# Two-layer hybrid trunk on one core: weight units rounded earlier, two low parts moved from GpSimd to VectorE, GpSimd's scalings moved behind two more units

## The reference

```python
def mixer_ab(h, w_in, ...):                      # layer 0
    u = h @ w_in                                 # pool | z | xbc | dt
    xbc = silu(causal_dwconv(xbc, conv_w) + conv_b)      # 4 taps
    ...                                          # chunked scan, gate with silu(z), norm
    return concat([pool_out, y]) @ w_out

def mixer_cd(h, w_in, dw_w, dw_b, ln_g, ln_b, sc_w, w_out):   # layer 1
    u = h @ w_in                                 # a | gate | bg | cg | hh, 1024 channels each
    v = u[a] * sigmoid(u[gate])
    v = causal_dwconv(v, dw_w) + dw_b            # 31 taps, 1024 channels
    conf_out = silu(layernorm(v) * ln_g + ln_b)
    sc_out = u[bg] * causal_dwconv(u[cg] * u[hh], sc_w)       # 3 taps
    return concat([conf_out, sc_out]) @ w_out
```

## Time and profile before

| | us |
|---|---|
| median of 3 runs | 904.92 |
| lowest, highest | 904.24, 906.71 |
| profiled execution, its own time | 906.82 |
| its span, first to last instruction | 905.1 |

### The profile page before, as it was taken

How to read it: one execution, slowest core, us unless ns; L and a number is a source line. 1 busy time by engine, 2 the same in 40 slices (tenths; PEclk the granted TensorE clock), 3 DMA queues, 4 the chain that set the end, 5 groups by cost and what they waited for, 6 DMA issues and landing times.

```text
span 905.1 us, 14746 instructions
## 1 busy us (share of the span) xinstructions
PE 877.0 (97%) x6078; PEld 801.9 (89%) x6078; DVE 622.7 (69%) x961; ACT 477.7 (53%) x697; POOL 176.0 (19%) x163
## 2 busy tenths in 40 slices
PE   8999998999999999999998999999999899999997
PEld 7899986899889999999898999787999799999996
DVE  4786996596576655555589999966587475555554
ACT  6664564565465544444564443357575555444443
POOL 1120710000000000000009888667200000000000
PEclk9999999999999999999999999999999999999999
DMA  8454434553455555665565676344552456565551
GB/s 294 146 179 147 136 103 155 167 185 120 149 179 187 189 187 194 193 191 187 185 178 168 197 216 195 126 150 155 183 164 93 141 186 211 189 192 195 190 188 70
DMA packets 82954, 155.27 MB, mean 172 GB/s; under 512 B 6838, under 2 KB 8776, under 8 KB 82888
## 3 DMA queue, kind: packets, MB, share of 16 engines
q1 hardware_dynamic: 82776, 154.29, 53.4%
q10 hardware_dynamic: 112, 0.05, 0.0%
HBM read 152.11 MB, written 1.05 MB: 169 GB/s over the span
## 4 chain that ended last, share of the span: by engine, by line
PE 74%; DVE 14%; ACT 4%; DMA 2%; POOL 2%; SPq 1%; issue 1%; DVEq 0%; POOLq 0%; ACTq 0%
PE ps L557 13%; PE ps L558 13%; PE ps L559 13%; PE ps L624 10%; PE ps L626 10%; PE ps L625 10%; DVE w_lo L1544 4%; ACT w_hi L1120 2%; DVE ps L1901 2%; DVE cv L2080 1%; DVE xT L1823 1%; POOL w_lo L2204 1%; DMA raw<-in_ab_w_in 1%; DVE h_lo L1555 1%; DVE xc L1611 1%
## 5 line engine op out<-in xcount | busy, mean ns | idle before, releaser
L1120 ACT ACTIVATE w_hi<-raw 128x1024 fp32r<-128x1024 f32 x284 | 295.1, 1054 | 220.9 <-DMA raw<-in_mlp_w 128.7
L1544 DVE TENSOR_TENSOR w_lo<-raw,w_hi 128x1024 fp32r<-128x1024 f32 x238 | 286.9, 1227 | 125.7 <-ACT w_hi L1120 124.9
L557 PE MATMUL ps<-h_hi,w_hi 128*128 128x256 f32 x1120 | 316.1, 282 | 10.4 <-POOL w_lo L2204 6.0
L558 PE MATMUL ps<-h_lo,w_hi 128*128 128x256 f32 x1120 | 313.9, 280 | 0.0
L559 PE MATMUL ps<-h_hi,w_lo 128*128 128x256 f32 x1120 | 313.7, 280 | 0.0
L557 PEld LDWEIGHTS ps<-h_hi,w_hi 128*128 128x128 f32 x1120 | 212.3, 190 | 13.8 <-POOL w_lo L2204 6.7
L559 PEld LDWEIGHTS ps<-h_hi,w_lo 128*128 128x128 f32 x1120 | 213.7, 191 | 0.0
L558 PEld LDWEIGHTS ps<-h_lo,w_hi 128*128 128x128 f32 x1120 | 212.0, 189 | 0.6
L2233 POOL TENSOR_TENSOR rfac<-stat,mhalf 128x1 f32<-128x1 f32 (+2 forms) x18 | 15.7, 872 | 624.5 <-DVE stat L1797 507.0
L2204 POOL TENSOR_TENSOR w_lo<-raw,w_hi 128x1024 fp32r<-128x1024 f32 x46 | 114.7, 2517 | 23.4 <-ACT w_hi L1120 23.4
L624 PE MATMUL ps<-w_hi,r_hi 128*128 128x512 f32 x256 | 99.8, 390 | 0.0
(11 more groups left out here) (274 smaller groups left out, 1237.7 us busy)
## 6 DMA issues: line engine op xcount, KB each, us to landing
raw<-in_mlp_w SPq DMA_DIRECT2D x128, 512.0 KB, 3.8
raw<-in_cd_w_in SPq DMA_DIRECT2D x40, 512.0 KB, 4.0
raw<-in_xa_wkv SPq DMA_DIRECT2D x32, 512.0 KB, 3.8
raw<-in_ab_w_in SPq DMA_DIRECT2D x24, 512.0 KB, 4.6
raw<-in_xa_wq SPq DMA_DIRECT2D x16, 512.0 KB, 3.6
raw<-in_xa_wo SPq DMA_DIRECT2D x16, 512.0 KB, 3.8
raw<-in_cd_w_out SPq DMA_DIRECT2D x16, 512.0 KB, 3.6
raw<-in_ab_w_out SPq DMA_DIRECT2D x12, 512.0 KB, 3.7
```

The lines of the kernel that those rows point to most:

```text
L557: nc.tensor.matmul(dst, wt[0], x[0], start=start, stop=False, skip_group_check=True)
L558: nc.tensor.matmul(dst, wt[0], x[1], start=False, stop=False, skip_group_check=True)
L1120: nc.scalar.activation(w_hi[:, v % SLOTS, :, :], raw[:, v % SLOTS, :, :], ACT.Copy)\
L1544: V.tensor_tensor(w_lo[:, v % SLOTS, :, :], raw[:, v % SLOTS, :, :], f(w_hi[:, v % SLOTS, :, :]), ALU.subtract).then_inc(lo_ready_dve, 1)
```

## The change

Four edits, all to the order of work or to who does it; nothing that is computed changes.

1. `pool_lo` begins two units later: the low parts of units 148 and 149 go from GpSimd to VectorE.
2. ScalarE rounds unit 7 ahead of the first taps of the 4-tap convolution, and VectorE takes its low part ahead of `conv4(0)` and no longer inside it.
3. ScalarE rounds units 18 and 19 each ahead of a silu instead of behind it, and VectorE takes unit 19's low part right behind `conv4(5)`.
4. GpSimd's four scalings of the 3-tap convolution (line 2324) stand two units later in its list: behind units 169, 171, 177 and 179 instead of 167, 169, 175 and 177.

```diff
@@ pool_lo
-    for u in range(first[("gate", 1)], first[("out", 1, "late", 0)]):
+    for u in range(first[("gate", 1)] + 2, first[("out", 1, "late", 0)]):
         pool_lo[u] = u % 8 != 7
@@ ScalarE, layer 0
             own()
+            round_to(F_[("xbc", 1)] + 3)
             first_taps(0)
             first_taps(1)
@@
-            for i in range(4, 6):
-                silu_pair(i)
-                round_to(F_[("z", 1)] + i - 2)
+            round_to(F_[("z", 1)] + 2)
+            silu_pair(4)
+            round_to(F_[("z", 1)] + 3)
+            silu_pair(5)
@@ VectorE, layer 0
-            conv4(0, {2: F_[("xbc", 1)] + 3})
+            low_to(F_[("xbc", 1)] + 3)
+            conv4(0, {})
             conv4(1, {1: F_[("xbc", 2)]})
@@
             conv4(5, {2: F_[("z", 1)] + 2})
+            low_to(F_[("z", 1)] + 3)
@@ GpSimd, layer 1
                             i = 2 * g + q
-                            low_to(F_[("hh", g)] + 3 + 2 * q + 4)
+                            low_to(F_[("hh", g)] + 9 + 2 * q)
                             pool.wait_ge(dve_made, after("dve", "cv3", i))
```

## The result

The changed kernel takes 909.88 us (median of 8 runs, 907.52 to 915.75) where the kernel before takes 905.78 (8 runs beside them, 904.24 to 907.19). The ratio is 1.0054, with a 95% interval of 1.0038 to 1.0069: slower, by 4.1 us between the medians and 4.9 by the ratio, in which the one execution of 915.75 weighs more. The profiled execution took 910.76, with a span of 909.0.

What follows compares the result with a forecast made beforehand. In layer 1's mixer TensorE has only a short lead over a VectorE that never rests. 906.82 - 4.5 (early edits) + 7.1 (lateness) + 1.7 (clock) = 911.1, taken as a median of 910.0 us; range 899.0 to 914.0.

Steps and rivals of the forecast that it cites:

- the mechanism at edit 4: 3-tap convolution: GpSimd never stands still, so VectorE waits turns and TensorE starts unit 178 7.1 us later; chance 0.50.
- the sum: Whole kernel: 906.82 - 4.5 + 7.1 + 1.7 = 911.1 us own time, median taken as 910.0.
- the open point of that step: Unit 7: the 2.13 us gain needs its weights landed by 27.5 or so; no row showed the landing.
- the turns: 3-tap convolution: GpSimd takes its turn after each VectorE instruction; pair 1 makes VectorE 3.8 us late.
- The stall of 1.73 stays in full: TensorE at unit 170: unit 171 ready at 542.9, as late as before, so nothing gained there.
- TensorE is 5.5 us late: Unit 175's low part, behind pair 2 on VectorE, ready near 559.9; the stall costs another 1.7 of clock.
- the other sum of the same step: End of the mixer: VectorE's last addition, 10 us late, ends at 605.7, beside TensorE's own 606.1.
- it takes its turn: 3-tap convolution: GpSimd, never standing still, gets in after each VectorE instruction, which then waits for it.
- The 1.7 us of clock in the sum: Full-speed time lost to a lower clock behind the long TensorE stall for unit 175.
- Rival A: Mixer of layer 1: the turns don't add up, VectorE meets GpSimd less, all four stalls go; 899.8 us, chance 0.28.
- Rival B: 3-tap convolution: one round of turns only, pair 1 pays 3 us, pair 2 escapes; 905.0 us, chance 0.22.
- The rule behind it: VectorE instructions with two SBUF inputs wait in full for GpSimd reading SBUF: 910; without it 899.8.

Runs made afterwards that it cites:

- a3: The kernel before with only GpSimd's scalings of the 3-tap convolution two units later: 915.04 us, ratio 1.0103.
- a2: The changed kernel with GpSimd's scalings of the 3-tap convolution back in their old places: 902.22 us, ratio 0.9958.
- a1: The kernel before with only units 7 and 19 rounded and split ahead: 902.13 us, ratio 0.9964.
- a4: The kernel before with only the low parts of units 148 and 149 on VectorE: 905.65 us, ratio 1.0005.
- b1: The changed kernel with VectorE taking unit 175's low part before pair 2 opens instead of behind its 3-tap instructions: 909.36 us, ratio 1.0040.
- b3: The changed kernel with only the scalings of pairs 0 and 1 late, those of pairs 2 and 3 in their old places: 905.54 us, ratio 0.9998.
- b2: The changed kernel with five of GpSimd's low parts beside the 3-tap convolution replaced by a fill that reads nothing: 899.50 us, ratio 0.9924.
- b4: a2 with GpSimd's units 155 and 156 before the scaled sigmoids, VectorE taking 175 early and 179 behind pair 3, ScalarE rounding 179 early: 903.53 us.
- c1: b4 with VectorE taking unit 159 ahead of a(1,0), 175 behind the five taps of pair 2, and 178 instead of 179: 900.33 us, ratio 0.9937.
- d2: c2 with unit 171's low part on VectorE behind pair 1: 901.21 us, ratio 0.9940.
- d1: c1 with unit 171's low part on VectorE behind pair 1: 904.41 us, ratio 0.9975.
- c2: c1 with five 31-tap instructions behind the first 3-tap instruction of pairs 1 and 3: 901.25 us, ratio 0.9943.

## Why the prediction was right

**The forecast, slower by the mechanism at edit 4, held:** 910.0 said, 909.88 measured, own time 911.1 said and 910.76 measured. a3 prices edit 4 by itself at 9.1 us, after against a2 at 7.7 by the medians and 8.7 by the ratios; the sum had 7.1 + 1.7 = 8.8, with edit 1's 0.7 in it. That the median was met within 0.1 us is partly luck: 910.0 was worked out beside 904.92 for before, a change of 5.1, and the change is 4.1 beside 905.78.

**Edit 2 and edit 3.** Said 4.5, and 5.1 in the profiled execution. Unit 7's rounding began at 25.31 and its low part ran from 27.11 to 28.32, where the prediction had it ready near 29.0; the unit had landed in time, the open point of that step. In the medians (a1) it is 3.8.

**Edit 1.** Said between -0.6 and +1.0, taken +0.7; a4 measures +0.5 by the ratio, with an interval of about -0.7 to +1.7, and -0.3 by the medians. The first product of the gate stage came 1.65 late (473.50 + 5.09 against 476.94), as said (1.8), and the stalls of 1.17 and 1.08 are the form that this took. The prediction had unit 156 0.2 us late; it came 0.2 early (497.74 + 5.1 against 503.05).

**Edit 4, the turns.** Pair 1: 7.8 said, 7.36 measured, with GpSimd busy throughout. Pair 2: one turn, 4.2 said (1.79 + 2.4), 3.87. Pair 3: three waits, 7.9 said (1.8 + 2.4 + 1.3 + 2.4), 6.97. The number of turns is as said; the sizes are not. Behind a low part an instruction took 2.1 to 2.2 us longer than by itself, behind a scaling 0.9, where the sum took a whole 2.4 and 1.3, and pair 1's first instruction lost 0.4 behind unit 168. The three pairs cost 2.6 + 2.1 + 2.2 = 6.9 us more than before, where 3.1 + 2.4 + 3.1 = 8.6 was said. VectorE also came to pair 1 0.1 us late in the time of before (527.08 + 5.1 against 532.05), not 0.7.

**What was wrong in it.** "The stall of 1.73 stays in full": it fell to 0.17. Unit 171 was ready at 536.71, which is 541.8 in the time of before and not 542.9, and TensorE, held up by the two new stalls in the gate stage, came later. "TensorE is 5.5 us late" at unit 175: it was 7.52. TensorE wanted the unit 0.9 us earlier than said, mostly because the stall of 1.73 had gone, and the low part was ready at 555.78 + 5.1 = 560.9 and not 559.9. And the clock stood at half for some 10 us, 5.1 us of full-speed time, not 1.7. None of the three moved the end. For the long stall b1 shows it: with 1.03 in its place the time is nearly the same. For the others it follows from after's trace, where TensorE, with all three in it, still waits 0.32 us for VectorE at the sum. The end was set by the other sum of the same step, VectorE's last addition, said for 605.7 in the time of before and measured at 601.23 + 5.1 = 606.3.

**That this sum came out is in part luck.** It had the pairs and the start too dear, by 1.7 and 0.6 us, and left out the addition `Ssum` between pairs 1 and 2, which costs 2.2. So the first bg product came at 565.14 + 5.1 = 570.2, as said (570.1), by errors that cancel. VectorE's lateness can be added up from instructions: it came to pair 1 5.0 us ahead of before and ended its last addition 5.6 behind, and these 10.5 us are the pairs (6.85), `Ssum` behind pair 1 (2.18), the low part of the first bg product (0.96) and a later `Ssum` (0.55). The addition behind pair 1 takes 2.85 to 2.88 us in a3, b1 and b3, and 0.70 to 0.75 in a1, a2, a4, b2, b4 and c1. The step "it takes its turn" holds for it too; that it would meet a low part was not foreseen.

**The clock.** The 1.7 us of clock in the sum was right only by luck: behind VectorE it was free, and another loss of 1.6 us, at 722 us, stood in its place in this execution.

**Rival A** falls with pair 1 at 7.36 us. **Rival B's** mechanism is real, and its size came out: 3.3 us (b3 against a2), though b3's trace has the long `Ssum` beside pair 1. It lost because pair 2 did not escape: unit 176 was rounded from 549.75 to 550.79, in time for GpSimd to meet pair 2's second instruction at 551.17.

**The rule behind it.** The Trainium skill, SBUF — State Buffer, section "Who interferes with whom", has a VectorE instruction with two SBUF inputs and a GpSimd one that reads SBUF exclude each other. The traces agree, now with the row of turns that the trace of before did not have (7.36 us for four instructions), and with b2's fill, which only writes and excludes nothing (0.47 us beside it).

## What to carry to other kernels

Where instructions of two engines exclude each other, as here, an engine's waits are part of the other's speed: moving GpSimd's wait out of a stretch filled the stretch with turns, and cost VectorE 2.1 to 2.6 us in each pair and 2.2 more in an addition between them. Before filling an idle engine, look at what runs free beside its idleness; and where turns can't be avoided, put instructions with an input in PSUM between those that take turns, so that the waiting is worked through (d2 against d1, 3.2 us). It pays only where VectorE is waited for: c2 against c1 gained nothing.

A long stall isn't a price by itself. If the engine that caused it is late in any case, curing the stall moves it (b1): follow the late engine to the last place where it is waited for.

## What the runs showed that I had not expected

**Who goes first in a tie is not fixed.** At unit 159 the two low parts start 0.05 to 0.09 us apart in seven profiled executions, GpSimd's first each time. In six of them (after, a2, a4, b1, b2, b4) VectorE ran free and GpSimd waited; in b3, at 0.07, it was the other way round and VectorE lost 2.2 us. The distance alone does not decide it. The 2.2 us are more than half of what the whole change is worth and may be a part of the spread of one kernel's runs (b3's go from 904.31 to 909.64); this was not tried.

**The clock does not follow the length of a stall.** Behind 1.97 us it fell to half in a1 (0.83 over ten microseconds), behind 2.50 in b3, while behind 3.02 in b4 it stayed full:

```profile
500.00:510.00 10.00, 6.98 (x59) 6.81 (x59) 10.00 (x24) 3.22 (x5) 10.00 (x4) 1.00 0.27 75
```

TensorE rests 3.0 of these 10 us and the granted clock is 1.00. What decides it stays open; a sum should carry the clock as a term of either 0 or 1.7 us for a stall of 2 to 3 us.

**Work on VectorE costs more than its length.** Where it bounds the stage, 1.22 us more of it cost 3.4 to 4.1 (d1), with a stall of 2.96 at a unit that had been in time. Another 2.17 of it are one addition that the shift moved onto a low part of GpSimd (0.70 in c1, 2.87 in d1). A shift of VectorE's work is priced only when each instruction behind it that has two SBUF inputs has been held against GpSimd's list.
